# Block mixer: outputs of pairs 0 and 1, and of pairs 2 and 3, issued together, scores ahead of outputs

## The reference, cut to what matters

```
qkv = (h @ w_qkv).reshape(B, S, 3, H, hd)
q = rmsnorm(qkv[:, :, 0], q_gain); k = rmsnorm(qkv[:, :, 1], k_gain); v = qkv[:, :, 2]
lo = einsum('bhnid,bhnjd->bhnij', qb, kb) * SCALE
lo = where(ii >= jj, lo + own_bias, NEG)
p = exp(lo - max(lo)); o = einsum(eq, p / sum(p), v)
return o.astype(h.dtype) @ w_o
```

## Time and profile before

| | us |
|---|---|
| median of three runs | 904.14 (903.77 to 904.65) |
| the profiled execution | 903.69 |
| its span, first to last instruction | 901.9 |
| TensorE matmul busy | 893.8 (99%) |
| TensorE weight load busy | 766.3 (85%) |
| VectorE busy | 624.6 (69%) |
| ScalarE busy | 488.9 (54%) |
| GpSimd busy | 40.2 (4%) |

### The profile page before, as it was taken

How to read it: one execution, slowest core, us unless ns; L and a number is a source line. 1 busy time by engine, 2 the same in 40 slices (tenths; PEclk the granted TensorE clock), 3 DMA queues, 4 the chain that set the end, 5 groups by cost and what they waited for, 6 DMA issues and landing times.

```text
span 901.9 us, 13857 instructions
## 1 busy us (share of the span) xinstructions
PE 893.8 (99%) x5614; PEld 766.3 (85%) x5614; DVE 624.6 (69%) x1084; ACT 488.9 (54%) x733; POOL 40.2 (4%) x69
## 2 busy tenths in 40 slices
PE   9999999999999999999999999999999999999998
PEld 7987888987888888877999988888877799998886
DVE  5679877779977998785766644456788586664441
ACT  7555747555747754565555543346567465554330
POOL 2600010000000000000000000000000000000000
PEclk9999999999999999999999999999999999999999
DMA  8953454632445478632565555657464265555540
GB/s 296 324 191 98 137 187 145 228 100 95 140 141 184 145 250 251 182 109 86 155 188 190 189 197 177 221 164 231 123 206 126 93 227 187 188 188 188 185 162 24
DMA packets 79455, 155.55 MB, mean 172 GB/s; under 512 B 5656, under 2 KB 7864, under 8 KB 79392
## 3 DMA queue, kind: packets, MB, share of 16 engines
q1 hardware_dynamic: 75200, 142.81, 48.5%
q0 software_dynamic: 4192, 11.85, 4.9%
HBM read 153.54 MB, written 1.11 MB: 171 GB/s over the span
## 4 chain that ended last, share of the span: by engine, by line
PE 85%; DVE 8%; ACT 4%; issue 1%; DMA 1%; SPq 0%; DVEq 0%; ACTq 0%
PE ps L755 17%; PE ps L757 17%; PE ps L756 16%; PE ps L786 8%; PE ps L787 7%; PE ps L788 7%; DVE w_lo L1881 3%; ACT w_hi L1396 1%; PE ps_mid L965 1%; PE ps_mid L981 1%; PE ps L1056 1%; DVE area L2382 1%; ACT y_tok L1522 1%; PE ps_mid L951 1%; DMA w_raw<-in_w_in 1%
## 5 line engine op out<-in xcount | busy, mean ns | idle before, releaser
L1881 DVE TENSOR_TENSOR w_lo<-w_raw,w_hi 128x2048 fp32r<-128x2048 f32 x133 | 299.9, 2260 | 156.8 <-ACT w_hi L1396 156.6
L1396 ACT ACTIVATE w_hi<-w_raw 128x2048 fp32r<-128x2048 f32 x133 | 250.9, 1890 | 189.4 <-PE ps L757 139.0
L755 PE MATMUL ps<-w_hi,act_hi 128*128 128x512 f32 (+1 forms) x446 | 178.1, 399 | 0.3
L757 PE MATMUL ps<-w_hi,act_lo 128*128 128x512 f32 (+1 forms) x446 | 171.2, 384 | 0.0
L756 PE MATMUL ps<-w_lo,act_hi 128*128 128x512 f32 (+1 forms) x446 | 170.9, 383 | 0.0
L755 PE MATMUL ps<-w_hi,hid 128*128 128x512 f32 x296 | 116.3, 393 | 0.1
L757 PE MATMUL ps<-w_hi,hid 128*128 128x512 f32 x296 | 115.4, 390 | 0.0
L756 PE MATMUL ps<-w_lo,hid 128*128 128x512 f32 x296 | 115.3, 389 | 0.0
L786 PE MATMUL ps<-act_hi,w_hi 128*128 128x256 f32 x384 | 110.8, 289 | 0.4 <-DVE act_lo L2080 0.4
L787 PE MATMUL ps<-act_lo,w_hi 128*128 128x256 f32 x384 | 107.6, 280 | 0.0
L788 PE MATMUL ps<-act_hi,w_lo 128*128 128x256 f32 x384 | 107.5, 280 | 0.0
(11 more groups left out here) (369 smaller groups left out, 1239.4 us busy)
## 6 DMA issues: line engine op xcount, KB each, us to landing
w_raw<-in_ffn_w SPq DMA_DIRECT2D x64, 1024.0 KB, 5.3
w_raw<-in_w_in SPq DMA_DIRECT2D x21, 1024.0 KB, 6.0
w_raw<-in_a_w_qkv SPq DMA_DIRECT2D x18, 1024.0 KB, 5.0
w_raw<-in_b_w_qkv SPq DMA_DIRECT2D x12, 1024.0 KB, 5.1
w_raw<-in_w_out SPq DMA_DIRECT2D x8, 1024.0 KB, 4.9
w_raw<-in_b_w_o SPq DMA_DIRECT2D x4, 1024.0 KB, 5.0
w_raw<-in_w_in SPq DMA_DIRECT2D x12, 256.0 KB, 5.9
w_raw<-in_w_in SPq DMA_DIRECT2D x4, 512.0 KB, 3.6
```

Of the source, the lines that this page charges most:

```text
L755: pe.matmul(o, ah, wh, start=first, stop=False)
L757: mm = pe.matmul(o, al, wh, start=False, stop=last)
L1396: act.activation(w_hi[:, c % RING, :, 0:n], w_raw[:, c % RAW, :, 0:n], ACT.Copy).then_inc(w_hi_done, 1)
L1881: dve.tensor_tensor(lo, w_raw[:, c % RAW, :, 0:n], hi.bitcast(F), ALU.subtract).then_inc(w_lo_done, 1)
```

## The change

TensorE no longer issues the output of a pair after each odd unit. A table `BLOCK_OUT` says after which unit which outputs come: pairs 0 and 1 after unit 3, pairs 2 and 3 after unit 7, pairs 4 to 7 after units 9, 11, 13 and 15 as before. Where scores and outputs stand at the same unit, the scores now come first. The transposes of pair 4 move from the end of unit 5 to just ahead of the transposes of unit 6. ScalarE and VectorE take the high and low parts at the start of the unit that follows the outputs. VectorE's split `splits(f + 5, 1)` moves from the hook of unit 10 to that of unit 12. Nothing is computed differently.

```diff
+        BLOCK_OUT = {3: (0, 1), 7: (2, 3), 9: (4,), 11: (5,), 13: (6,), 15: (7,)}
@@ block_attention, TensorE
                     ahead(BLOCK_A[u])
+                    if u == 6:
+                        stage_pair(3, BLOCK_STAGED[5])
                     block_transposes(u)
                     if u in BLOCK_STAGED and u != 5:
                         stage_pair(3, BLOCK_STAGED[u])
                     ahead(BLOCK_B[u])
-                    if u % 2:
-                        block_output(u // 2)
-                    if u == 5:
-                        stage_pair(3, 4)
                     if u in BLOCK_SCORES:
                         block_scores(BLOCK_SCORES[u])
+                    for q in BLOCK_OUT.get(u, ()):
+                        block_output(q)
@@ units, ScalarE
-                    if ph == 3 and u and u % 2 == 0:
-                        pair_high(u // 2 - 1)
+                    if ph == 3:
+                        for q in BLOCK_OUT.get(u - 1, ()):
+                            pair_high(q)
@@ units, VectorE
-                    if ph == 3 and u and u % 2 == 0:
-                        pair_low(u // 2 - 1)
+                    if ph == 3:
+                        for q in BLOCK_OUT.get(u - 1, ()):
+                            pair_low(q)
@@ block_attention, VectorE: table of hooks
-                ... 7: lambda: splits(f + 5, 0), 10: lambda: splits(f + 5, 1), 13: ...
+                ... 7: lambda: splits(f + 5, 0), 12: lambda: splits(f + 5, 1), 13: ...
```

More of the change, by code:

```diff
@@ L2319, in hook5 @@
                     splits(f + 4, 1)
-                units(3, MOBA_HEADS, {1: hook1, 2: lambda: splits(f + 3, 1), 3: lambda: splits(f + 4, 0), 4: hook4, 5: hook5, 7: lambda: splits(f + 5, 0), 10: lambda: splits(f + 5, 1), 13: lambda: splits(f + 6, 0)})
+                units(3, MOBA_HEADS, {1: hook1, 2: lambda: splits(f + 3, 1), 3: lambda: splits(f + 4, 0), 4: hook4, 5: hook5, 7: lambda: splits(f + 5, 0), 12: lambda: splits(f + 5, 1), 13: lambda: splits(f + 6, 0)})
                 pair_low(7)
```

## The result

The changed kernel takes 905.67 us (median of 20 runs) against 904.12 us, a ratio of 1.0015 with a 95% interval of 1.0009 to 1.0021, that is 0.8 to 1.9 us slower. The forecast was 905.3. The profiled execution took 905.66 us around a span of 903.9, before 903.69 around 901.9.

The account below looks back on a forecast made before the run. TensorE was taken to bound the kernel, VectorE close behind. New waits of 2.36 us, less 0.77 old waits, 0.10 entry and 0.30 joins, gave +1.2 on 904.14: 905.3 us, 8-in-10 range 904.3 to 906.2.

Parts of the forecast that it names:

- the chain that was named: VectorE's in-order list from pair 1's subtraction: starts 0.52 us late, holding logits 6 and the normalization behind it.
- fifth pair's transposes: At unit 6, TensorE waits 1.10 us for VectorE's late normalization; start forecast at 676.17.
- scores 5: At unit 7, scores without output 3 ahead wait 0.77 us for the sixth pair's copy; start 683.30.
- unit 13's copy: On VectorE, 0.2 us late behind the moved split; output 6's 0.6 us slack covers it, otherwise up to 0.5.
- The old waits: TensorE's waits at units 5 and 11 in the kernel before, 0.28 and 0.49 us, would go: 0.77 saved.
- the entry: One place fewer with outputs or scores, eight instead of nine, since unit 5 has none left: about 0.10 us saved.
- rival 4: At unit 11, the moved split has no effect because scores' 0.85 us cover the wait; inside the forecast, 0 us.
- The joins: Where outputs of pairs 0 and 1, and 2 and 3, stand together: 0.15 us saved each, 0.30 in all.
- the wait at unit 12: The projection's second half waits 0.27 us until logits 15 have left its PSUM bank.
- Rival 1: Not slower: the normalization is in time at unit 6, all four new waits go, 1.17 us gained, 903.0; chance 0.08.
- Rival 2: Half the loss: scores at unit 7 find their copy, 0.77 less, +0.45, 904.6 us; chance 0.14.
- Rival 3: More loss: unit 13's copy too late, or score-to-output seams dearer and no saving from adjacent outputs; +1.7 to +1.9; chance 0.18.

Follow-up runs that it names:

- logits-first kernel: Changed kernel, but at unit 4 VectorE does logits 6 and 7 before subtracting pairs 0 and 1; 904.23 us, ratio 1.0002 to the kernel before.
- outputs-first kernel: Changed kernel, but at units 3, 7, 9 and 11 TensorE issues outputs ahead of scores again; 903.62 us, ratio 0.9994.
- split-back kernel: Changed kernel with VectorE's split back at unit 10 instead of unit 12; 905.36 us, one run.
- one output a unit: Changed kernel, but pairs 0 to 3 are output after units 1, 3, 5 and 7, still behind the scores; 905.23 us, ratio 1.0013.
- transposes back: Changed kernel with the fifth pair's transposes returned to the end of unit 5; 906.37 us, one run.
- both cures: Changed kernel with VectorE's logits before subtractions at units 4 and 12, and outputs before scores at unit 7 alone; 903.31 us, ratio 0.9991.

## Why the prediction was right

The forecast was +1.2 us on the chain that was named; the rows give +1.35 in the mixer and the timing +1.55 (0.8 to 1.9). By its own steps, in the clock of the kernel before (0.61 us less than the rows):

| step | forecast | measured |
|---|---|---|
| pair 1 subtracted | 669.98 | 669.92 |
| fifth pair's transposes start, wait | 676.17, 1.10 | 676.12, 1.12 |
| unit 6's transposes start, wait | 676.82, 0.22 | 676.78, 0.23 |
| scores 5 start, wait | 683.30, 0.77 | 683.30, 0.76 |
| dense work after unit 7 | 685.60 | 685.61 |
| the projection's second half starts, wait | 701.9, 0.27 | 701.95, 0.29 |
| unit 13's copy behind the moved split | 704.0, covered | 704.02, covered |

- **The cause** is shown by the logits-first kernel (1.11 us back from one exchange in VectorE's list) and by the outputs-first kernel (1.93 us back).
- **The old waits**, 0.28 and 0.49 us: the second is measured as 0.49 by the split's move alone. The first was not taken by itself; with the 0.10 of the entry the sum has 0.38, and the starts give 0.40. (From unit 5's transposes to the first dense matmul behind unit 6's it is 4.27 us before and 4.49 after; less output 2's 0.80 and the new waits, 3.47 and 3.07.) That the move is worth nothing in the new order, rival 4, is shown by the split-back kernel.
- **The joins.** Two outputs took 1.60 us and now take 1.46 (684.76 to 686.22), 0.14 to 0.15 a join, as taken. Only my sign for it in the rows was wrong: the starts are 0.70 apart, not 0.65, because 0.10 of the gain is on leaving the first output and 0.05 inside the second.
- **Where it was short**, by 0.15 us in the mixer: two waits cost more than their length, which the sum did not have. The projection's first matmul after its wait, at 702.56, takes 0.34 us to the next start instead of 0.23, and unit 6's transposes after theirs take 0.31 (677.39 to 677.70) instead of 0.24. The waits themselves are 2.40 where the sum has 2.36; with 0.11 and 0.07 and less 1.17 that makes 1.41, against 1.35 measured. The other way goes a gain that no term has: at unit 3's transposes, before any wait, the changed kernel is 0.85 us ahead (665.20 less 0.61 against 665.44), where one output less gives 0.80; no run shows why. That the total came so close is in part these two in opposite directions. What is left between 1.35 and the 1.55 of the timing lies within its interval.
- **A slip in the working**: the wait at unit 12 by its own terms is 701.9 less 701.65, 0.25 and not 0.27; the rows have 0.29.
- **Rival 1** (the normalization in time) is out; it is what the logits-first kernel brings about at unit 6. **Rival 2** is out: scores 5 waited 0.76. **Rival 3** is out: the outputs kept their slack and the seams of both directions cost the same.

The rule of the Trainium skill that VectorE's queue is strictly in order ("TensorE: Matmul & The Clock Gate", Part 1, Architectural detail) agrees with the trace: logits 6, ready for over 1 us, start only 0.34 us after the subtraction of pair 1. The Trainium skill also says that a change of the tiling mode drains TensorE and a change of the tile alone does not ("TensorEngine Tiling (Array Packing)", Key Properties). The trace agrees in its numbers: a second output behind the first saves 0.15 us, and each entry from dense work costs 0.09.

## What to carry to other kernels

Before an instruction of the bound engine is moved later, look for who reads its result, and what stands behind that reader in its list: here an output that nobody needed soon held back a normalization that was needed at once. Where two engines work near their limit, put the short work whose input is ready ahead of the one that waits. A wait that goes by covering it and one that goes by moving its cause are the same 0.49 us; count it once.

## What the runs showed of the hardware that I had not expected

A dense matmul that follows a wait takes some 0.11 us more to the next start than in a stream, with the clock granted in full. It is the same 0.34 us that the first dense matmul behind a group of outputs or scores takes without any wait (658.34 to 658.68 in the kernel before). The transposes after a wait took 0.06 to 0.07 us more.

The start of the mixer wanders by 1.5 us between the profiled executions, one of each kernel, though no edit touches anything ahead of it: 637.2 us at the earliest (one output a unit), 638.7 at the latest (transposes back). Behind the mixer nothing wanders: to the last instruction it is 185.1 us in all nine. In the kernel before, the stretch 0 to 40 us reads:

```profile
0.00:40.00 40.00, 38.80 (x226) 33.12 (x227) 24.77 (x28) 26.30 (x35) 17.30 (x32) 1.00 0.90 305
```

and with the transposes back:

```profile
0.00:40.00 40.00, 38.55 (x221) 32.99 (x222) 24.78 (x28) 25.75 (x35) 16.81 (x32) 1.00 0.90 300
```

The DMA engines are 0.90 busy there and TensorE gets less done in the second. Compared by the same matmul of the program, this stretch holds nearly all of the wandering in the other kernels (1.0 us for both cures, whose mixer starts 1.04 late), but with the transposes back only 0.5 of 1.3 us; the rest falls between 430 and 530 us. That the weights' arrival is the cause was not tested, and the second part is unexplained. The wandering is as large as what was studied, which is why the timing alone could separate only the slower kernels here.
